# A wider spacing of pick steps among the u products, and a pick written in fewer instructions, in a hybrid attention and expert layer on one Trainium2 core

## What is computed

```python
q = (xp @ w_pq).reshape(m, PEER_HEADS, 2, PEER_HALF)
s = jnp.einsum("thpc,pnc->thpn", q, sub_keys).astype(jnp.float32)
hs, hi = lax.top_k(s, PEER_TOPK)                       # 16 of 128 keys, twice per head
cand_s = (hs[:, :, 0, :, None] + hs[:, :, 1, None, :])  # 256 sums
cand_i = (hi[:, :, 0, :, None] * PEER_NKEYS + hi[:, :, 1, None, :])
best_s, pos = lax.top_k(cand_s, PEER_TOPK)
idx = jnp.take_along_axis(cand_i, pos, axis=-1)         # 8 heads x 16 experts per token
gate = jax.nn.softmax(best_s, axis=-1)
a = jnp.einsum("thkd,td->thk", peer_u[ib], xb)          # ib, gb: idx, gate
act = jax.nn.gelu(a, approximate=False) * gb
out = jnp.einsum("thk,thkd->td", act, peer_v[ib])
```

## Time and profile before

| | us |
|---|---|
| median of 3 runs | 2872.45 |
| lowest and highest run | 2862.47, 2876.3 |
| the profiled execution | 2873.59 |
| its span, first to last instruction | 2870.4 |
| busy: PE | 2103.8 |
| busy: DVE | 1889.7 |
| busy: POOL | 1254.6 |
| busy: ACT | 473.5 |

### The profile page before, as it was taken

How to read it: one execution, slowest core, us unless ns; L and a number is a source line. 1 busy time by engine, 2 the same in 40 slices (tenths; PEclk the granted TensorE clock), 3 DMA queues, 4 the chain that set the end, 5 groups by cost and what they waited for, 6 DMA issues and landing times.

```text
span 2870.4 us, 19586 instructions
## 1 busy us (share of the span) xinstructions
PE 2103.8 (73%) x6070; PEld 1063.1 (37%) x6070; DVE 1889.7 (66%) x2681; ACT 473.5 (16%) x1107; POOL 1254.6 (44%) x854
## 2 busy tenths in 40 slices
PE   7999999999999898978899900000331038999996
PEld 3665444444545443333344400000331035444443
DVE  1212000386687756656576899999999998666666
ACT  1212100112222210101001100000993034000000
POOL 2000000034354444434353367666688865454444
PEclk9999999999999999999999955555555558999998
DMA  9777688989999989999999999999999988999999
GB/s 364 273 287 257 222 288 305 314 330 373 362 395 402 395 343 411 404 387 413 402 370 368 412 366 390 380 382 374 354 419 421 422 335 281 409 405 406 408 409 353
DMA packets 271464, 1047.10 MB, mean 365 GB/s; under 512 B 19856, under 2 KB 19856, under 8 KB 203280
## 3 DMA queue, kind: packets, MB, share of 16 engines
q0 software_dynamic: 113792, 697.85, 60.8%
q1 hardware_dynamic: 154880, 343.97, 32.9%
q10 hardware_dynamic: 2704, 4.21, 0.4%
HBM read 1036.50 MB, written 9.45 MB: 364 GB/s over the span
## 4 chain that ended last, share of the span: by engine, by line
PE 40%; DMA 24%; DVE 21%; POOL 8%; issue 6%; ACT 1%; SPq 0%; DVEq 0%; POOLq 0%; ACTq 0%
PE ps L587 35%; DMA yTr<-in_peer_v,fold 12%; DVE bigs L1583 7%; POOL bigr L558 6%; DMA bigr<-in_w_br_a 4%; DVE bigr L1583 3%; DVE hr L1613 3%; DMA bigr<-in_w_out 2%; DMA bigs<-in_peer_v,idxnow 2%; DMA bigr<-in_w_in 2%; DVE spare L1583 2%; POOL spare L558 1%; DVE pwork L1390 1%; DMA bigs<-in_peer_u,idxnow 1%; PE ps L648 1%
## 5 line engine op out<-in xcount | busy, mean ns | idle before, releaser
L587 PE MATMUL ps<-bigr 128*128 128x512 f32 x1920 | 857.6, 605 | 44.9 <-DMA bigr<-in_w_in 19.6
L587 PEld LDWEIGHTS ps<-bigr 128*128 128x128 f32 x1920 | 367.3, 194 | 495.1 <-issue 443.5
L511 POOL DMA_INDIRECT bigs<-in_peer_u,idxnow x128 | 238.4, 1862 | 560.8 <-DVE bigs L1530 543.8
L587 PE MATMUL ps<-bigr,bigs 128*128 128x512 f32 x896 | 404.4, 605 | 23.0 <-DMA bigr<-in_w_in 19.4
L1613 DVE SCALAR_TENSOR_TENSOR hr<-yTr,fold,hr 128x1024 f32<-128x1024 f32 x205 | 263.0, 1283 | 132.9 <-DMA yTr<-in_peer_v,fold 131.9
L1520 DVE SCALAR_TENSOR_TENSOR bigs<-bigs,acts 128x2048 f32<-128x2048 f32 x128 | 300.7, 2349 | 59.9 <-DMA bigs<-in_peer_v,idxnow 59.7
L1530 DVE SCALAR_TENSOR_TENSOR bigs<-bigs 128x2048 f32<-128x2048 f32 x128 | 293.0, 2290 | 68.9 <-DMA bigs<-in_peer_u,idxnow 67.8
L568 POOL DMA_INDIRECT yTr<-in_peer_v,fold x205 | 214.4, 1046 | 215.3 <-DVE hr L1613 205.1
L1583 DVE SCALAR_TENSOR_TENSOR bigr<-bigr 128x2048 f32<-128x2048 f32 x122 | 278.1, 2290 | 14.7 <-DMA bigr<-in_peer_u,fold 13.9
L558 POOL DMA_INDIRECT bigr<-in_peer_u,fold x122 | 252.9, 2073 | 64.3 <-issue 34.0
L852 PE MATMUL ps<-ident,fold 128*128 128x128 f32 x2 | 1.0, 476 | 375.9 <-DVE fold L1589 375.9
(11 more groups left out here) (260 smaller groups left out, 2219.4 us busy)
## 6 DMA issues: line engine op xcount, KB each, us to landing
bigr<-in_w_in SPq DMA_DIRECT2D x160, 1024.0 KB, 9.2
spare<-in_peer_v SPq DMA_DIRECT2D x96, 512.0 KB, 6.7
bigr<-in_w_out SPq DMA_DIRECT2D x32, 1024.0 KB, 6.7
bigr<-in_w_pq SPq DMA_DIRECT2D x32, 1024.0 KB, 8.0
bigr<-in_w_br_a SPq DMA_DIRECT2D x16, 1024.0 KB, 9.6
bigr<-in_w_br_b SPq DMA_DIRECT2D x16, 1024.0 KB, 9.8
bigr<-in_peer_v SPq DMA_DIRECT2D x32, 512.0 KB, 6.7
bigr<-in_ckT_a POOLq DMA_DIRECT2D x2, 2048.0 KB, 10.4
```

Source lines behind the costliest of these rows:

```text
L511: pool.indirect_dma_start(row, None, table[:, :], bass.IndirectOffsetOnAxis(ap=col, axis=0)).then_inc(loaded, 16)
L587: last = mm(ps[:, bank + t, :], src[:, k0 + k, t * P:(t + 1) * P], wring[:, s, k, :], start=(k0 + k == 0), stop=(k0 + k == kt - 1))
```

## The change

Three edits, in one diff. (1) In the loop of the u products a pick step stands behind each fourth product (k = 3, 7, ...) and no longer behind each third. The 52nd step then stands behind product 207, the 208th. (2) `places`: the subtraction of the best sums is done once for all eight heads, in the last part; the two lists of ranked key numbers are one list of 33 entries (`numbered`), written by one bitwise or and one copy, where it took two bitwise ors and a copy; `ranks` holds both runs of ranks for that and is written by two instructions on POOL. (3) `name`: the number of the expert is written straight into the integer tile, and the doubled one is made from that and also written as an integer, so the two copies are gone.

```diff
-CONSTS = 15
+CONSTS = 16
...
-        ranks = sb("ranks", [P, TOPK + 1], U32)
+        ranks = sb("ranks", [P, 2 * TOPK + 1], U32)
...
+        numbered = pwork[:, 256:256 + 2 * (2 * TOPK + 1)].bitcast(U32).rearrange("p (h k) -> p h k", h=2)
+        ranked = [numbered[:, :, 0:TOPK + 1], numbered[:, :, TOPK + 1:2 * TOPK + 1]]
...
-            link(pool.iota(ranks[:, :], pattern=[[RANK, TOPK + 1]], base=0, channel_multiplier=0))
+            pool.iota(ranks[:, 0:TOPK + 1], pattern=[[RANK, TOPK + 1]], base=0, channel_multiplier=0).then_inc(made, 1)
+            pool.iota(ranks[:, TOPK + 1:], pattern=[[RANK, TOPK]], base=0, channel_multiplier=0).then_inc(made, 1)
...
-                        link(dve.tensor_copy(bmax[:, r], best[:, r, 0]))
-                        last = dve.tensor_tensor(best[:, r, :], best[:, r, :],
-                                                 bmax[:, r].unsqueeze(2).to_broadcast([P, ph, TOPK]), ALU.subtract)
                         if i == parts - 1:
-                            last.then_inc(best_ready, 1)
-                        else:
-                            step(last)
+                            link(dve.tensor_copy(bmax[:, :], best[:, :, 0]))
+                            dve.tensor_tensor(best, best, bmax[:, :].unsqueeze(2).to_broadcast([P, PH, TOPK]),
+                                              ALU.subtract).then_inc(best_ready, 1)
...
-                        step(dve.tensor_tensor(ranked[0][:, :, 1:TOPK + 1], both[:, :, 0, :],
-                                               ranks[:, 1:TOPK + 1].unsqueeze(1).to_broadcast([P, ph, TOPK]),
+                        step(dve.tensor_tensor(numbered[:, :, 1:], both,
+                                               ranks[:, 1:].unsqueeze(1).to_broadcast([P, ph, 2 * TOPK]),
                                                ALU.bitwise_or))
-                        step(dve.tensor_copy(ranked[0][:, :, 0], both[:, :, 0, 0]))
-                        step(dve.tensor_tensor(ranked[1], both[:, :, 1, :],
-                                               ranks[:, 0:TOPK].unsqueeze(1).to_broadcast([P, ph, TOPK]),
-                                               ALU.bitwise_or))
+                        step(dve.tensor_copy(numbered[:, :, 0], both[:, :, 0]))
...
-                        link(dve.scalar_tensor_tensor(cijf[:, 0, slots], rows_, float(P), cols, ALU.mult, ALU.add))
+                        last = dve.scalar_tensor_tensor(eidx[t][:, slots], rows_, float(P), cols, ALU.mult, ALU.add)
                         if F.streams:
-                            dve.tensor_copy(eidx[t][:, slots], cijf[:, 0, slots]).then_inc(picked, 1)
+                            last.then_inc(picked, 1)
                         else:
-                            step(dve.tensor_copy(eidx[t][:, slots], cijf[:, 0, slots]))
-                            link(dve.tensor_scalar(cijf[:, 1, slots], cijf[:, 0, slots], 2.0, 1.0, ALU.mult, ALU.add))
-                            dve.tensor_copy(hidx[:, t, slots], cijf[:, 1, slots]).then_inc(picked, 1)
+                            link(last)
+                            dve.tensor_scalar(hidx[:, t, slots], eidx[t][:, slots], 2.0, 1.0, ALU.mult, ALU.add
+                                              ).then_inc(picked, 1)
...
-                if k % 3 == 2 and len(stages) > 1:
+                if k % 4 == 3 and len(stages) > 1:
```

More of the change, by code:

```diff
@@ L262, in build @@
         kval = pwork[:, 0:256].rearrange("p (b k) -> p b k", k=TOPK)
-        ranked = [pwork[:, 256 + n * 40:256 + n * 40 + 2 * (TOPK + 1 - n)].bitcast(U32).rearrange("p (h k) -> p h k", h=2)
-                  for n in range(2)]
+        numbered = pwork[:, 256:256 + 2 * (2 * TOPK + 1)].bitcast(U32).rearrange("p (h k) -> p h k", h=2)
+        ranked = [numbered[:, :, 0:TOPK + 1], numbered[:, :, TOPK + 1:2 * TOPK + 1]]
         kidx = pwork[:, 512:768].bitcast(U32).rearrange("p (b k) -> p b k", k=TOPK)
@@ L447, in _ @@
             link(pool.tensor_scalar_mul(ntriB[:, :], triB[:, :], -1.0))
-            link(pool.iota(ranks[:, :], pattern=[[RANK, TOPK + 1]], base=0, channel_multiplier=0))
+            pool.iota(ranks[:, 0:TOPK + 1], pattern=[[RANK, TOPK + 1]], base=0, channel_multiplier=0).then_inc(made, 1)
+            pool.iota(ranks[:, TOPK + 1:], pattern=[[RANK, TOPK]], base=0, channel_multiplier=0).then_inc(made, 1)
+            order.value += 2
+            pool.wait_ge(made, order.value)
             link(pool.memset(maskC[:, :], 0.0))
```

2 lines of the change are left out of this document (1 added, 1 removed).

## The result

The changed kernel takes **2849.46 us** (median of 8 runs, 2843.16 to 2856.95); the kernel before takes 2874.59 us beside it (8 runs, 2862.47 to 2878.71). The ratio is 0.9932 with a 95% interval of 0.9913 to 0.9952: 19.5 us less, between 13.8 and 25.0. The two medians as they stand lie 25.1 us apart, which is the upper end of that interval: eight runs of a kernel that scatters by 14 to 16 us say no more than that. The forecast was 2855 us with a gain of 18.9 us. The profiled execution takes 2852.17 us with a span of 2850.3, 20.1 us less than the 2870.4 before.

The account below looks back on a forecast made before the run. DVE was taken to bound the loop while steps are mixed in, the gathers afterwards. Gains of 14.3 + 3.3 + 1.3 = 18.9 us from 2873.6 left 2854.7; forecast 2855 us, with 2847 to 2866 to hold 8 in 10.

Parts of the forecast that it names:

- What bounds the loop: Loop of products: DVE bounds it while steps are mixed in, then the gathers, with 0.276 us of waiting a product.
- Edit 1: Loop of products: wider spacing leaves 48 products behind the last step, 39 waiting, 10.8 us in place of 25.1; gain 14.3 us.
- The wait on `picked`: POOL, ahead of the gathers of certain slots: the later-named parts still come in time, so no gather is held.
- ScalarE's cover: Tile 1's best sums come some 110 us later, but ScalarE waited 146.9 us for product 255, so nobody waits.
- `places`, 0.37 us a part: Pick step `places`: each part saves 0.37 us, bounds 0.2 to 0.45; a tile's last part gains nothing.
- `name`, 0.30 us: Pick step `name`: its middle instructions go, saving 0.30 us of 0.92, from 0 to 0.4.
- Ahead of the loop, 1.3 us: Last stream experts: parts 0 and 1 of tile 0 save 2 x 0.67 = 1.3 us, DVE having no gap there.
- rival (d): Front of `R`: the earlier streams' pick shifts the phase of gathers against DVE, total 2846 to 2864 us; chance 0.10.
- The last stretch moves whole: From the last product to the end: 540 us, starting from the same state of rings and queues, moves as a whole.
- (a): Tile 1's six buffers bind, products wait between steps: 12 us lost, gain 7, time 2866 us; chance 0.10.
- (b): Loop gathers already get all that the DMA gives, 2.78 us each with steps; slower, 2898 us; chance 0.04.
- (c): The spacing works and the small edits do not: 14.3 us alone, time 2859 us; chance 0.10.

Follow-up runs that it names:

- e6: The changed kernel with the tile's finish and the first two quads' marks moved among the last products; 2848.48 us, ratio 0.9933 to the kernel before.
- e7: The changed kernel with the edits of e5 and e6 together; 2846.54 us, ratio 0.9927 to the kernel before; 2843.93 us in a second execution.
- e4: The changed kernel with five buffers in place of six for tile 1's gathers; 2855.56 us, ratio 0.9953 to the kernel before.
- e1: The kernel before with only the spacing changed, a step behind each fourth product; 2851.54 us against 2868.51, ratio 0.9949.
- e3: The changed kernel with a step behind every second product; 2868.18 us, ratio 1.002 to the kernel before.
- e2: The changed kernel with the old spacing, so the small edits alone; 2865.16 us, ratio 0.9994 to the kernel before.
- e5: The changed kernel with the 52 steps spread over 217 products; 2846.85 us, ratio 0.9932 to the kernel before; 2845.67 us in a second execution.
- e11: e7 with three v rows added before the third quad's marks instead of one; 2841.73 us, ratio 0.9907 to the kernel before.
- e8: The changed kernel unaltered, executed a third time; 2847.40 us.

## Why the prediction was right, point by point

**What bounds the loop.** Right. DVE bounds it while steps are mixed in, and the gathers' rate bounds it afterwards. e6 and e7 show the second half directly: 3.3 us of work put there cost the loop nothing. e4 shows that it is the rate and not the round of a buffer.

**Edit 1, 14.3 us.** Right, by e1 a little more: 15.0. At the end of every loop without moved work a product follows the last one after 2.485 to 2.489 us, 0.27 us more than the 2.215 without a wait; e3, with 117 waits, was 6.5 us off mainly by their number. The size that was off is the lead behind the last step. I took nine products from the trace of before. In the three traces of the changed kernel the first product that waits is number 215, 217 and 219, so the lead is seven, nine and eleven products; it is eleven in e1, eight in e2 and ten in both traces of e5's kernel. The nine was a good middle of something that varies between executions of one kernel, each product of it worth 0.276 us. In e3 it is some 34, in the ring of eight.

**The wait on `picked`.** Right: no product before 215 waits for a gather. e5 moved the last part's number nine products further, and no wait appeared between its steps either.

**ScalarE's cover.** Right. It still waits for the last product, 115.1 us where it had 146.9. Nobody else is late. But the chain that begins with it turned out to be the next bound: in e6, e7 and e11 the third quad's marks start 5.1 to 5.2 us behind the last product, whatever DVE has ready.

**`places`, 0.37 us a part.** Wrong in the loop, right ahead of it. In the loop the step saves 0.17 us three times (1.30 to 1.13) and 0.38 once (1.51 to 1.13; there, in the trace before, the next product waits 0.2 us more for the step's own last instruction): I had given the copy of two columns 0.19 to settle, and it lasts 0.35 there. Among the stream experts it lasts 0.16, and the step saves 0.36 and 0.35. A last part takes 1.35 us (2160.97 to 2162.32), 0.05 more than before, near the 0.03 that I set to 0.

**`name`, 0.30 us.** Too low in the loop, right ahead of it. In the loop it saves 0.48 (0.92 to 0.44, in five of six parts): I let the middle instructions go and kept the last cast with its 0.40 us up to the next product. The instruction that is last now lasts 0.18 us and lets the product start after 0.22. Among the stream experts the step took 0.74 and takes 0.44. All in all the small edits save 3 x 0.17 + 0.38 - 2 x 0.05 + 5 x 0.48 + 0.3 = 3.5 us in the loop; e2 measured 3.1. That the prediction's 3.3 comes so near is luck in part: two misses of opposite sign cancel.

By the rule that I had weighed against this, from the Trainium skill's page "Vector Engine (DVE) Microarchitecture Reference", section 5.2, it would have been 2.5 us. The 3.1 us measured are nearer to the sum from the rows. In the rows of `name` above each of the two instructions takes its 0.22 us, and the second needs the first's result. By the figures of that page of the Trainium skill it would be about 0.11 us for 32 columns, an estimate from its 75 ns and 1.04 ns a column; the trace has twice that.

**Ahead of the loop, 1.3 us.** The steps there are shorter by just that (0.36 + 0.35 for `places`, twice 0.30 for `name`). Whether the loop starts sooner for it is not decided. It starts 2.4 us earlier after the change, but the start lies anywhere from 1639.9 to 1661.9 us in these traces, and for the changed kernel alone at 1654.6, 1650.8 and 1639.9. In the three traces of the changed kernel it carries 14.7 of the 16.0 us by which the spans differ. Two rows from the traces of e8, which starts its loop at 1639.9, and of e5, at 1661.9, for 1200 to 1500 us:

```profile
1200.00:1500.00 300.00, 262.92 (x605) 115.04 (x604) 196.68 (x152) 21.94 (x34) 137.94 (x90) 0.96 1.01 403
```

```profile
1200.00:1500.00 300.00, 256.97 (x585) 111.98 (x584) 188.79 (x146) 21.94 (x34) 136.12 (x86) 0.95 0.98 389
```

Where the transfers, gathers of stream experts beside weights, run at 389 GB/s and not at 403, the front of `R` is through later. That is only half of it. Instruction for instruction on DVE, e5 lies 3 us behind e8 at 1200 us, 14 at 1500 and 22 at 1600. The rest comes from one wait for TensorE in the front of `R`, of the first trace after the change and of e8:

```profile
1529.58 1.29 DVE L1365 TENSOR_TENSOR hr<-ps,hr 128x512 f32<-128x512 f32 x2 [12.66 <-PE ps L590]
```

```profile
1514.09 1.29 DVE L1365 TENSOR_TENSOR hr<-ps,hr 128x512 f32<-128x512 f32 x2 [0.70 <-PE ps L590]
```

These two run the same kernel and with the same 402 to 403 GB/s from 1200 to 1500 us, and their lead of 5 us at 1500 becomes 15 at 1600. In twelve of the fourteen traces, that of before among them, DVE waits 7.5 to 12.7 us there, and the transfers nearly stop for some 10 us (to 8 and 1 GB/s in slices of 3.5 us after the change). In e6 and e8 the wait is 0.8 and 0.7 us, the transfers go on, and the loop starts early (1646.8 and 1639.9). What makes the wait long or short was not tried. That the phase of the streams' pick sets it, as rival (d) has it, is not shown; the scatter is there in every kernel, changed or not.

**The last stretch moves whole.** Right for the change: 540.8, 540.6, 540.5 and 540.4 us in the trace before and the three after. It is not a law. In single traces it is 2 to 4 us longer, with dips in the rate of the transfers.

**The rivals.** (a), the six buffers bind: refuted, no wait between steps, 9.3 us to landing. But e4 shows that it is real with five: 8.5 us. (b), the gathers already had all the rate: refuted, 405 GB/s with steps mixed in, from 1800 to 1900 us as well as in tile 1, where I had found 377. The note of the Trainium skill that I named there ("DMA: Bandwidth & Descriptors", section Bandwidth) holds HBM transfers to about 358 GB/s a core; by the 422 GB/s above it is not a limit here. The table of measured transfers on that page of the Trainium skill, for a core whose neighbour is idle, has 425 GB/s for its largest one, and with that the trace agrees. (c), the small edits are worth nothing: refuted by the loop of e2, though its median, 3.4 us below before, could not tell. (d) is right that the front of `R` scatters, its cause open.

**The total.** The loop was to take 653 to 657 us and takes 655.05. The median, 2849.46, is 5.5 us below the forecast, well inside the 22 us over which the loop's start lies in these traces; the ratio, 0.9932, is that of the forecast's sum (2854.7 of 2873.6, 0.9934). What shows the mechanism is the loop, 17.55 us shorter where 17.6 were forecast; that the whole came as near is luck in part, for the start alone moves a run by more.

## What to carry to other kernels

Where a loop changes its bound halfway, side work belongs evenly into it, up to the point where the other bound takes over: count the iterations that wait, and multiply by the wait with its hand-over; don't count on the total of idle time. Work moved into a wait is free, but it helps only if what stands behind the wait was late because of that work; follow the chain of the last result through the other engines before moving anything. And when an edit is worth a few us of 2850, compare the stretch in the trace: the loop repeated within 0.1 to 1.1 us, while runs of one kernel scattered by up to 26.

## What had not been expected of the hardware

- The same small instruction of DVE lasts twice as long in the loop of products as among the stream experts: the copy of two columns 0.35 us (four times in the trace above) against 0.16, the last cast of the old `name` 0.37 against 0.18 at the least. In a tile's last part it does not hit that copy. What makes the difference is open.
- With one buffer fewer, a gather of 1 MiB lands after 9.0 us and not 11.5 at the same 422 GB/s: the time to landing counts what is in the queue, not how fast it moves.
- The same kernel moves its last 183.4 MB in 463.2 us once and in 465.9 another time, with slices of some 12 us in which the rate falls from 409 to 380 GB/s.
